# A two-block layer stack on one core: x turned among the last head's steps, joined output weights, attention tables issued by the sync engine, four stage barriers of the tensor engine less

## The reference, cut to what matters

```python
def hybrid_layer(x, w_in, ..., w_hy_out, w_rw_out, w_o, ln1_w, ln1_b, ffn_w_gate, ffn_w_up, ffn_w_down, ln2_w, ln2_b):
    proj = x @ w_in
    u_h, u_r, gates = jnp.split(proj, [HY_COLS, HY_COLS + RW_COLS], axis=-1)
    y_h = hyena_mixer(u_h, ...) @ w_hy_out          # 512 channels to 1024
    y_r = rwkv_mixer(u_r, ...) @ w_rw_out           # 512 channels to 1024
    g_h, g_r = jnp.split(jax.nn.sigmoid(gates), 2, axis=-1)
    mix = (g_h * y_h + g_r * y_r) @ w_o
    x = layer_norm(DN_ALPHA * x + mix, ln1_w, ln1_b)
    ffn = (jax.nn.silu(x @ ffn_w_gate) * (x @ ffn_w_up)) @ ffn_w_down
    return layer_norm(DN_ALPHA * x + ffn, ln2_w, ln2_b)
```

## Time and profile before

| | us |
|---|---|
| median of 3 runs | 2673.92 |
| profiled execution, its own time | 2676.65 |
| its span | 2674.8 |
| PE busy | 2446.4 (91%) |
| PEld busy | 1980.2 (74%) |
| DVE busy | 1051.3 (39%) |
| ACT busy | 826.0 (31%) |
| POOL busy | 799.4 (30%) |
| mean granted clock of PE | 0.961 |

### The profile page before, as it was taken

One profiled execution on the slowest core, in us unless ns is written; L12 is line 12 of the kernel. 1 busy time (PEld: TensorE's weight loads), 2 busy tenths in 40 slices (PEclk: granted clock), 3 DMA queues, 4 the chain that ended last, 5 costly groups with the idle time before them and its releaser, 6 DMA issues.

```text
span 2674.8 us, 42640 instructions
## 1 busy us (share of the span) xinstructions
PE 2446.4 (91%) x17856; PEld 1980.2 (74%) x17856; DVE 1051.3 (39%) x1640; ACT 826.0 (31%) x1192; POOL 799.4 (30%) x394
## 2 busy tenths in 40 slices
PE   6978988787989999997999999999998869999999
PEld 5547776676778887885568887787777758888787
DVE  3554465543215223034435322033288854322023
ACT  3212444323322222122342222122255532222122
POOL 2122222223543444341023444342000013444333
PEclk9989898898999999998999999999999979999999
DMA  6102100002342333332012333232221103333322
GB/s 173 55 16 74 48 4 4 3 16 79 87 123 70 101 95 94 103 118 77 1 55 72 94 96 100 103 101 92 79 64 48 56 32 87 96 100 94 102 95 87
DMA packets 256280, 200.16 MB, mean 75 GB/s; under 512 B 13782, under 2 KB 235709, under 8 KB 255744
## 3 DMA queue, kind: packets, MB, share of 16 engines
q1 hardware_dynamic: 239744, 177.23, 22.1%
q10 hardware_dynamic: 16384, 20.70, 2.4%
HBM read 195.80 MB, written 2.10 MB: 74 GB/s over the span
## 4 chain that ended last, share of the span: by engine, by line
PE 73%; DVE 12%; issue 6%; ACT 4%; POOL 2%; ACTq 1%; PEld 1%; DVEq 1%; DMA 0%; PEldq 0%; POOLq 0%
PE psum_banks L292 19%; PE psum_banks L293 19%; PE psum_banks L294 19%; POOL weights_lo L271 2%; PE psum_banks L1815 2%; PE psum_banks L1005 2%; PE psum_banks L483 1%; PE psum_banks L490 1%; PE psum_banks L1840 1%; PE psum_banks L1582 1%; PE psum_banks L885 1%; PE psum_banks L1839 1%; DVE hgrn_buffer L2492 1%; DVE rwkv_buffer L1217 1%; DVE hgrn_buffer L2479 1%
## 5 line engine op out<-in xcount | busy, mean ns | idle before, releaser
L271 POOL TENSOR_TENSOR weights_lo<-weight_ring,weights_hi 128x1024 fp32r<-128x1024 f32 x270 | 645.3, 2391 | 1445.1 <-ACT weights_hi L260 1436.6
L292 PE MATMUL psum_banks<-x_by_channel_hi,weights_hi 128*128 128x512 f32 (+1 forms) x1632 | 631.0, 387 | 28.4 <-ACT hgrn_buffer L2258 14.5
L294 PE MATMUL psum_banks<-x_by_channel_hi,weights_lo 128*128 128x512 f32 (+1 forms) x1632 | 623.8, 382 | 0.0
L293 PE MATMUL psum_banks<-x_by_channel_lo,weights_hi 128*128 128x512 f32 (+1 forms) x1632 | 623.6, 382 | 0.0
L260 ACT ACTIVATE weights_hi<-weight_ring 128x1024 fp32r<-128x1024 f32 x278 | 294.2, 1059 | 1055.5 <-PE psum_banks L294 1046.3
L292 PEld LDWEIGHTS psum_banks<-x_by_channel_hi,weights_hi 128*128 128x128 f32 x1632 | 308.6, 189 | 98.6 <-ACT hgrn_buffer L2258 16.1
L294 PEld LDWEIGHTS psum_banks<-x_by_channel_hi,weights_lo 128*128 128x128 f32 x1632 | 308.4, 189 | 60.2
L293 PEld LDWEIGHTS psum_banks<-x_by_channel_lo,weights_hi 128*128 128x128 f32 x1632 | 308.9, 189 | 57.0 <-issue 0.2
L1672 DVE TENSOR_TENSOR hidden_lo<-ffn_buffer,hidden_hi 128x512 f32 (+1 forms) x66 | 122.2, 1851 | 413.2 <-ACT hidden_hi L1635 413.2
L292 PE MATMUL psum_banks<-weights_hi,hidden_hi 128*128 128x512 f32 x480 | 190.4, 397 | 12.8 <-DVEq L238 12.8
L1541 DVE SCALAR_TENSOR_TENSOR psum_banks<-x_by_token,psum_banks 128x1024 f32<-128x1024 f32 x24 | 29.4, 1224 | 407.7 <-PE psum_banks L294 407.6
(11 more groups left out here) (417 smaller groups left out, 3712.5 us busy)
## 6 DMA issues: line engine op xcount, KB each, us to landing
weight_ring<-in_ffn_w_in SPq DMA_DIRECT2D x88, 512.0 KB, 3.8
weight_ring<-in_ffn_w_down SPq DMA_DIRECT2D x66, 512.0 KB, 3.5
weight_ring<-in_w_in SPq DMA_DIRECT2D x43, 512.0 KB, 4.0
weight_ring<-in_hgrn_w_in SPq DMA_DIRECT2D x32, 512.0 KB, 4.0
weight_ring<-in_ffn_w_gate SPq DMA_DIRECT2D x22, 512.0 KB, 3.8
weight_ring<-in_ffn_w_up SPq DMA_DIRECT2D x22, 512.0 KB, 3.8
weight_ring<-in_ple_w_gate SPq DMA_DIRECT2D x16, 512.0 KB, 3.4
weight_ring<-in_w_o SPq DMA_DIRECT2D x8, 512.0 KB, 3.6
```

Of the source, the lines that this page charges most:

```text
L271: nc.gpsimd.tensor_tensor(wlo[:, j % SPLITS, :], ring[:, j % SLOTS, :], whi[:, j % SPLITS, :].bitcast(F32), ALU.subtract).then_inc(lo_done, 1)
L292: nc.tensor.matmul(bank, lh, rh, start=first, stop=False)
L293: nc.tensor.matmul(bank, lh, rl, start=False, stop=False)
L294: return nc.tensor.matmul(bank, ll, rh, start=False, stop=last)
```

## The change

1. **Last head.** For ht = 3 `steps_of` deals out 19 steps and not 12: the 12 post steps of head 2, and seven steps y, each of which splits one 512-column tile of the mixers' outputs (`y_high` on ACT, `y_low` on DVE, 128x512; PE has nothing to do in one). The gate product of the last head (post step 2 on PE) moves into the state steps, behind step 5.
2. **x.** SP loads x in four transfers of one token tile, as soon as the tables and the buffers under it are free. Four times eight transposes (`turn`), and their splits by token tile (`x_high`, `x_low`, 128x1024) stand among the last head's post steps.
3. **Mix stage.** w_hy_out and w_rw_out come in chunks of two output tiles (256 columns, 4 k-tiles), so that every chunk has 24 matmuls; 24 chunks and not 32. The order on PE is, for a pair of groups: hyena, hyena, gate h, gate r, rwkv, rwkv, gate h, gate r. The first two hyena products and the first two gate products stand in the stage before, ahead of the barrier. The loops are written out, and no longer rolled.
4. **Barriers.** In four stages (the norm of w_o and the three of the FFNs) PE drains and signals, but does not wait for the others; `starts` puts waits on semaphores ahead of single tiles in its place.
5. **Chunks 4 and 5 of each FFN's hidden stage** are split as soon as the first and second of the earlier chunks is done, two pieces sooner than before.
6. **Attention tables** are issued by SP behind the attention stage's last ring load, on the same condition, and the causal mask shares the weights' semaphore.

The core of the diff:

```diff
@@ stage_rwkv
+            if not ahead:
+                return [step for k in range(12) for step in ((("p", k, ht - 1), ("y", k // 2, None)) if k % 2 and k < 11
+                                                              else (("p", k, ht - 1),))] + [("y", k, None) for k in (5, 6)]
@@ act
-                for k in range(12):
-                    post_act(e, HT - 1, k)
+                tail["x_high"](e, 0)
+                post_act(e, HT - 1, 2)
+                tail["x_high"](e, 1)
+                post_act(e, HT - 1, 5)
+                tail["x_high"](e, 2)
+                post_act(e, HT - 1, 9)
+                tail["x_high"](e, 3)
+                tail["act_end"](e)
@@ pe
+                        if step == 5 and ht == HT - 1:
+                            e.wait_ge(r_kept, 2 * HT)
+                            post(ht, 2)
...
-                for k in range(12):
-                    post_pe(e, HT - 1, k)
+                tail["turn"](e, 0)
+                post_pe(e, HT - 1, 0)
+                tail["turn"](e, 1)
+                post_pe(e, HT - 1, 3)
+                tail["turn"](e, 2)
+                post_pe(e, HT - 1, 7)
+                tail["turn"](e, 3)
+                tail["pe_end"](e)
@@ stage_mix
+            def load(e, m):
+                n, kind = 2 * (m // 6), m % 6
+                if kind in (HH, RR):
+                    src = wr if kind else wh
+                    load_chunk(e, base, m // SLOTS, m % SLOTS, src[:, :, n * P:(n + 2) * P], two_tiles)
...
+            def sp(e):
+                for m in range(SLOTS):
+                    load(e, m)
+                may = {n: (s, v) for n, s, v in tail["x_may_come"]}
+                load_x(e, 0, may["channels"])
+                load_x(e, 1, may["masked"])
+                load_x(e, 2, may["levels"], may["masked"])
+                for m in range(SLOTS, SLOTS + 2):
+                    load(e, m)
+                load_x(e, 3, may["gate"], may["maps"])
+                for m in range(SLOTS + 2, 3 * DT):
+                    load(e, m)
...
+            def pe(e):
+                for n in range(0, DT, 2):
+                    if n:
+                        for h in range(2):
+                            hyena(e, n + h)
+                        for q in range(2):
+                            gate(e, n, q)
+                    for h in range(2):
+                        rwkv(e, n + h)
+                    for q in range(2):
+                        gate(e, n + 1, q)
...
+            def starts(e, k, tt):
+                if k == 0:
+                    if tt == 0:
+                        e.wait_ge(gate_sig, 2 * DT)
+                        e.wait_ge(mixed, DT - 2)
+                    elif tt == 1:
+                        e.wait_ge(second_half, DT)
+                elif tt == 0:
+                    e.wait_ge(mixed, min(DT, DT - 2 + k))
@@ stage_ffn_hidden
             def two_more(e):
                 for q in range(SPLITS):
-                    split_high(e, base, 1, q)
+                    n = base + TAIL + q
+                    e.wait_ge(weights_in[n % SLOTS], 16 * (n // SLOTS + 1))
+                    e.wait_ge(chunks_done, base + q + 1)
+                    nc.scalar.activation(whi[:, n % SPLITS, :], ring[:, n % SLOTS, :], ACT.Copy).then_inc(hi_done, 1)
...
+            def starts(e, k, tt):
+                if k == 0:
+                    if tt >= 2:
+                        e.wait_ge(hid, t0 + FT - 3 + tt)
+                    elif tt == 0:
+                        e.wait_ge(hid, t0 + FT - 2)
@@ run
-                    stage_barrier(me, eng, k)
+                    if me == "pe" and "starts" in part:
+                        eng.drain().then_inc(stage_done[me], 1)
+                    else:
+                        stage_barrier(me, eng, k)
```

291 lines of the change are left out of this document (196 added, 95 removed).

## The result

| | before | changed |
|---|---|---|
| median, us | 2672.93 (2671.69 to 2678.29, 4 runs) | 2608.73 (2599.92 to 2612.56, 4 runs) |
| profiled execution, its own time | 2676.65 | 2609.09 |
| its span | 2674.8 | 2607.3 |
| PE busy | 2446.4 (91%) | 2430.9 (93%) |
| mean granted clock of PE | 0.961 | 0.971 |

The ratio is 0.9758, 95% interval 0.974 to 0.9777: 2.4% faster. Forecast were 2604.1 us, in a range of 2598 to 2622.

What follows compares the result with a forecast made beforehand. PE was taken as the bound, so only its idle time at seams and the half clock behind it could be won. Six terms sum to 69.8 us off 2676.65: own time 2606.9, median 2604.1, range 2598 to 2622.

Steps and rivals of the forecast that it cites:

- the six terms: Gains at six places from last head to attention's entry: 15.3 + 9.0 + 6.3 + 19.2 + 3.0 + 17.0 = 69.8 us.
- the signs of being wrong: Low clock behind a shortened gap, PE waiting on tables or x, last-head levels over 2 us longer, total above 2622.
- A, seam: Last head to mix: hyena products start 17.4 us sooner, gate product costs 1.1; whole term 15.3 us, bounds 11 and 18.
- A, y splits: Seven y steps in the last head cost 1.0 us, between -1 and +4; already taken off the term's 15.3.
- My worst case of 2.84 for each: Rival: all seven y steps on the last head's chain at 2.84 cost 19.9 us, not 1.0; 2623 us, chance 4%.
- B: Mix stage: chunks of 24 matmuls hide the weight splits, saving 9.0 us; bounds 4 and 9.7.
- C: Mix to w_o: 4.0 us of gap and 2.3 of clock won, 6.3 us; bounds 3 and 6.7.
- D: Hidden to down, three times: 4.1 us of wait and 2.3 of clock each, 19.2 us; bounds 12 and 19.8.
- E: FFN hidden chunks 4 and 5: earlier splits remove PE's 1.3 us wait for ACT three times, 3.0 us; bounds 0 and 3.6.
- F: Entry of attention: ACT freed of its issues, 14.2 us of idleness and 2.8 of clock, 17.0 us; bounds 0 and 17.3.
- The rival that the half clock stays: New short waits at the same seams keep PE's half clock; 12.0 us less gain, 2616 us, chance 7%.
- The rival of late instructions in the written-out mix: PE's instructions come late in the mix stage, 1.6 us every 13 matmuls, costing 71 us; slower beyond that; chance 2%.

Runs made afterwards that it cites:

- gate_tail: Changed kernel with the last head's gate product back in the seam behind post step 0, not behind state step 5; 2603.69 us, ratio 0.9742.
- more_starts: Changed kernel with two more PE barriers, before mla_w_o and hgrn_w_o, replaced by waits ahead of single tiles; 2600.7 us, ratio 0.9732.
- split_old: Changed kernel with chunks 4 and 5 of each FFN's hidden stage split at the old place again; 2607.67 us, ratio 0.9753.
- unjoined: Changed kernel with w_hy_out and w_rw_out again in short chunks of 12 matmuls, in the new order; 2616.35 us, ratio 0.9794.
- barriers: Changed kernel with PE's barrier back ahead of the three FFN down stages; 2621.66 us, ratio 0.9817.
- barriers_warm: Changed kernel with the three FFN down barriers back and PE doing sixteen unread products in each wait; 2615.54 us, ratio 0.9796.
- tables_act: Changed kernel with the attention tables issued by ACT again at the old place, ahead of a high part; 2622.12 us, ratio 0.9814.
- the second series: The changed kernel measured once more with no edit, beside the kernel before; 2602.89 us, ratio 0.9749.

## Why the prediction was right, point by point

- **What bounds the kernel.** PE's idle time at seams and the half clock behind it were what could be won, and the six terms came out at 70.08 against 69.8. No rival came true. One of the signs of being wrong did: levels more than 2 us longer than the 48.03 of before. They were 1.67 longer in the first profile, but 2.15 to 2.54 in seven of the other ten with x early.
- **A, seam.** Right in sum, in part by luck: off in three sizes that cancel. I had the post chain pushed by 0.6 us and 1.1 more ahead of the first product. By the timeline the broadcast ends 6.65 us behind the start of the sum's last matmul, against 6.70 before, so it was not pushed at all. Nor is it in gate_tail, with the gate product in the seam again (6.7): PE's waits there had room for the first three batches either way. The product starts 0.8 behind the broadcast. The seam gave 18.33 and not 17.4. The gate product costs 0.91, forecast 1.1, and gate_tail shows it. (The state steps with the gate product among them took 7.63 to 7.79 in eight profiles, but 7.04 at a clock of 1.00 in more_starts and 8.42 at 0.64 in split_old.)
- **A, y splits.** Forecast was 1.0 us; the levels became 1.67 longer. The waits on DVE's L1258 grew by just the 1.0 that I had given (they are 1.1 to 2.6 us in the twelve profiles with the splits in the levels, 0.8 in the two without), and those on ACT fell by 0.6 (the root's step in a cheaper place, which I had named as a possibility). What the forecast had left out is that x's early transfers also fall into the levels: waits on issue grew by 0.6. PE's busy time grew by 0.7, and no run shows why. In the eleven profiles with x early the waits on issue are 5.2 to 7.0 us, with x late 3.1 and 4.7, in the kernel before 4.6: these don't overlap. The length of the levels is less clear (48.54 to 50.57 with x early, 47.80 and 49.44 late), since the clock and the waits on DVE move it too.
- **The port.** One y split of seven took 2.17 us, the others 0.68 to 0.86. My worst case of 2.84 for each was far off, since most fall where POOL is through. It is the same one, the fourth, in all twelve profiles with the splits in the levels: it overlaps POOL's L271 and takes 1.68 to 2.89 us.
- **B.** 8.73 for 9.0; unjoined shows that the joining carries it (11.36 in the new order, which alone would have lost 2.6). The split of the third pair, for which I left 0.6, makes no wait on POOL.
- **C and D.** 6.54 for 6.3 and 19.05 for 19.2. barriers gives back 18.8, and barriers_warm parts it into wait and clock and rules out contention.
- **E and F.** 3.13 for 3.0 and 16.88 for 17.0. split_old and tables_act bring back 3.1 and 16.8. (For the clock's part of F the sum has 2.8 where its own product gives 2.9.) The 4.4 us in front of the first attention product stayed, as said.
- **Clock and code.** The rival that the half clock stays had nothing for it: 31 matmuls in 7 us at 1.00 behind both kinds of shortened gap. The rival of late instructions in the written-out mix fell too: its 576 matmuls take 131.5 us, or 0.228 each.
- **The rest.** 2604.1 was forecast for the median and 2608.73 measured; the second series gave 2602.89. Of the 4.6 us between the first two, 2.2 are the profiled execution's (67.56 won, not 69.8); the other 2.4 come from the choice of executions, since the profile before lay 2.7 above its median and the changed one 0.4. The 2.5 us by which the profiled execution misses the sum lie in unedited stretches, whose scatter (6.7 us at the start of the last head) I had not priced. Whether all of it is scatter stays open: from its first product to hgrn_w_o the recurrence took 322.08 us before and 322.42 to 323.90 in the eleven changed kernels that keep that barrier, and of the kernel before there is one profile. The median is within the forecast's own range of 2598 to 2614.

## What to carry to other kernels

Where one engine is the bound, price a seam as its wait plus the slow clock behind it, and look for what exactly the first tile needs: a wait for that alone in place of a barrier gave back 6.3 us at each of three seams. Before moving DMA issues to another engine, look at what stands behind them in the issuer's list; moving them down in the same list gave nine tenths of the gain. Transfers that are started early to hide them are not free where the bound engine runs long unrolled code of small matmuls: look at its waits on issue before and after. Here that was worth about 1 us, too little to see in the times.

## What the runs showed of the hardware that I had not expected

- Four issues of a strided weight slice (w_uq) hold the issuing engine 10.5 to 14.9 us: 14.86 on ACT, 11.17 on SP, and 10.49 on ACT when issued 9 us later. They are far from equal: in tables_act the shortest took 0.6 and the longest 8.4 us.
- Sixteen products that nobody reads, 3.9 us of them, kept the clock at 1.00 through a barrier, at a DMA share of 0.68; without them the next 7 us ran at 0.76.
- Waits of PE on issue of up to 2.3 us each in the unrolled head, up to 7.0 us in one head, in which no semaphore is waited for. 114 of 116 of them end 2.2 to 2.9 us after a 16 KB packet of the instruction queue started. Where x's tiles filled the DMA queues at a share of 0.74, the next such packet came 6.3 us after the last, not 3.5 to 4.0, and PE waited 1.61 us.
